# A transformer block's first projection on the unnormed rows, with the norm's factor applied as its tiles leave PSUM

## The reference

```python
xn = rms_norm(h, norm_mix_pre[i])
z = xn @ w_in[i]
z_rwkv, z_gla = z[..., :RWKV_IN_WIDTH], z[..., RWKV_IN_WIDTH:]
...
qkv = jax.nn.silu(centred_dwconv(qkv, conv_w))
...
log_a = jax.nn.log_sigmoid(jnp.einsum('btdr,drc->btdc', a_lo, a_up) + a_b) / GLA_GATE_TEMP
...
o_f = gla_chunked(q_h, k_h, v_h, heads(log_a[:, :, 0], GLA_DK))
```

## Time and profile before

| | us |
|---|---|
| median of 3 runs | 2946.64 (2944.94 to 2954.29) |
| the profiled execution, its own time | 2958.57 |
| its span | 2956.7 |
| `load_constants` and `pre_norm` | 0 to 50.3 |
| `gla_project` | 50.3 to 208.8 |
| `gla_mix` | 208.8 to 327.7 |

### The profile page before, as it was taken

The page is one execution under the profiler, slowest core; times in us unless marked ns, Lnnn a source line. Parts: engine busy times, 40 slices in busy tenths (PEclk is TensorE's granted clock), DMA queues, the critical chain, the costliest instruction groups (busy, mean ns, idle before and its releaser), DMA issues.

```text
span 2956.7 us, 57419 instructions
## 1 busy us (share of the span) xinstructions
PE 2761.1 (93%) x24688; PEld 2261.2 (76%) x24688; DVE 1658.5 (56%) x2482; ACT 1220.4 (41%) x2232; POOL 355.9 (12%) x480
## 2 busy tenths in 40 slices
PE   4997899889998999899999999999999989999997
PEld 4776677788885777688888788788887768888876
DVE  5669676445454666556543437675446655654343
ACT  4776665222223454333333345432245433333331
POOL 2000123545440011101000000000001100100000
PEclk9997899899998999999999999999999999999998
DMA  4420344211101434333345232222323433334432
GB/s 142 136 75 3 103 140 166 64 38 40 39 20 37 137 135 164 130 123 125 118 146 177 87 108 92 89 95 94 100 93 128 164 122 131 121 114 152 165 121 86
DMA packets 138461, 319.27 MB, mean 108 GB/s; under 512 B 13344, under 2 KB 40608, under 8 KB 138208
## 3 DMA queue, kind: packets, MB, share of 16 engines
q1 hardware_dynamic: 115344, 236.94, 24.5%
q0 software_dynamic: 22864, 78.66, 7.6%
HBM read 268.23 MB, written 47.19 MB: 107 GB/s over the span
## 4 chain that ended last, share of the span: by engine, by line
PE 61%; DVE 3%; DMA 2%; ACT 1%; issue 1%; SPq 0%; POOL 0%; DVEq 0%; ACTq 0%
PE be_ps L3278 21%; PE be_ps L3204 16%; PE be_ps L3307 16%; PE be_ps L3257 7%; PE be_ps L3329 1%; DMA be_raw<-in_ffn_up 1%; DMA be_raw<-in_ffn_down 1%; PE be_ps L2784 1%; DMA ext<-f_first 1%; PE be_ps L2778 0%; DVE ext L2842 0%; ACT be_whi L3364 0%; PE be_ps L2411 0%; DVE big L2821 0%; DVE be_raw_r L3607 0%
## 5 line engine op out<-in xcount | busy, mean ns | idle before, releaser
L3607 DVE TENSOR_TENSOR be_raw_r<-be_raw,be_whi 128x1024 fp32r<-128x1024 f32 x229 | 280.6, 1225 | 502.0 <-ACT be_whi L3364 501.8
L3364 ACT CAST be_whi<-be_raw 128x1024 fp32r<-128x1024 f32 x229 | 240.2, 1049 | 608.2 <-DMA be_raw<-in_ffn_down 317.7
L3307 PE MATMUL be_ps<-ext_r,be_whi 128*128 128x512 f32 x1152 | 358.1, 392 | 4.6 <-ACT big L3370 4.6
L3278 PE MATMUL be_ps<-ext_r 128*128 128x512 f32 x832 | 280.9, 396 | 10.4 <-ACT be_ps L3425 10.4
L3204 PE MATMUL be_ps<-ext_r,be_whi 128*128 128x512 f32 x896 | 278.9, 393 | 5.8 <-DVE be_raw_r L3607 3.1
L3307 PEld LDWEIGHTS be_ps<-ext_r,be_whi 128*128 128x128 f32 x1152 | 217.6, 189 | 50.5 <-ACT big L3370 5.5
L3278 PE MATMUL be_ps<-mid_r,ext_r 128*128 128x512 f32 x704 | 226.9, 398 | 10.2 <-ACT be_ps L3425 10.2
L3307 PE MATMUL be_ps<-ext_r,be_raw_r 128*128 128x512 f32 x576 | 225.7, 392 | 0.0
L3204 PEld LDWEIGHTS be_ps<-ext_r,be_whi 128*128 128x128 f32 x896 | 166.9, 188 | 45.4 <-DVE be_raw_r L3607 4.2
L3204 PE MATMUL be_ps<-big_r,be_whi 128*128 128x512 f32 x640 | 198.9, 392 | 0.0
L3278 PEld LDWEIGHTS be_ps<-ext_r 128*128 128x128 f32 x832 | 158.2, 190 | 48.0 <-issue 10.8
(11 more groups left out here) (412 smaller groups left out, 5545.6 us busy)
## 6 DMA issues: line engine op xcount, KB each, us to landing
be_raw<-in_ffn_down SPq DMA_DIRECT2D x88, 512.0 KB, 3.4
be_raw<-in_conv_in SPq DMA_DIRECT2D x48, 512.0 KB, 3.3
ext<-f_inner SPq DMA_DIRECT2D x72, 256.0 KB, 3.7
ext<-in_ffn_gate SPq DMA_DIRECT2D x30, 512.0 KB, 5.1
ext<-in_ffn_up SPq DMA_DIRECT2D x30, 512.0 KB, 4.3
gp_ada<-in_ada POOLq DMA_DIRECT2D x24, 512.0 KB, 3.7
rp_ada<-in_ada POOLq DMA_DIRECT2D x24, 512.0 KB, 4.2
be_raw<-in_ffn_gate SPq DMA_DIRECT2D x44, 256.0 KB, 2.8
```

Of the source, the lines that this page charges most:

```text
L3278: mm = pe.matmul(ps[:, bank], part[:, at], x, start=(not seeded and k == 0 and p == 0), stop=(k == 3 and p == 2), skip_group_check=True)
L3307: mm = pe.matmul(ps[:, steps.bank[n, g]], part[:, at], x, start=(i % NPAIR == 0 and u == 0 and p == 0), stop=(i % NPAIR == NPAIR - 1 and u ...
L3364: act.copy(w.hi[:, n % 3], w.raw[:, n % 3]).then_inc(w.hi_ready, 1)
L3607: dve.tensor_tensor(w.lo(n), w.raw[:, n % 3], w.hi[:, n % 3].bitcast(F32), ALU.subtract).then_inc(w.lo_ready, 1)
```

## The change

`load_constants` and `pre_norm` are gone. Their work is in the block of `gla_project`, in class `FirstNorm`. x is loaded in eight pairs of half tiles; `xn_hi` and `xn_lo` are now made of x times the gain, without the token's factor, and the projection's tile 0 starts on them tile by tile. The squares are made by ACT (five of eight tiles) and POOL (three), the factor is made as 128x1024 numbers (`scale`): PE sums with a matrix of ones between the products of tile 1, ACT takes the root, DVE the reciprocal. Every tile of the projection is now taken out of PSUM by DVE, which multiplies it by `scale`; before, ACT did that. The modulation's `per_step` is another tuple. In `gla_mix` POOL gets 32 instructions that add `xn_hi` and `xn_lo`, multiply by `scale` and split the result again, for `rwkv_project`; SP's second weight load waits for them. `k_factor` of `rwkv_project` uses the memory of `scale`.

```diff
-def pre_norm(core, w, source, h, gain, xn_hi, xn_lo, c, acc):
...
+class FirstNorm:
...
+    POOL_SQUARES = {0: (5, 6, 7), 1: (5, 6, 7)}
...
+    def load(self, sp, hf, q):
+        pair = slice(2 * q, 2 * q + 2)
+        sp.dma_start(self.h[:, pair, self.cols(hf)], self.source[:, pair, self.cols(hf)]).then_inc(self.loaded[hf][q], 16)
+    def hi(self, act, hf, m):
+        act.wait_ge(self.loaded[hf][m // 2], 16)
+        act.activation(self.xn_hi[:, m, self.cols(hf)], self.h[:, m, self.cols(hf)], ACT.Copy, scale=self.gain[:, m:m + 1]
+                       ).then_inc(self.hi_done, 1)
+    def lo(self, dve, hf, m):
+        dve.wait_ge(self.hi_done, KD * hf + m + 1)
+        dve.scalar_tensor_tensor(self.xn_lo[:, m, self.cols(hf)], self.h[:, m, self.cols(hf)], self.gain[:, m:m + 1],
+                                 self.xn_hi[:, m, self.cols(hf)].bitcast(F32), ALU.mult, ALU.subtract
+                                 ).then_inc(self.lo_done, 1)
+    def by_act(self, hf):
+        return [m for m in range(KD) if m not in self.POOL_SQUARES[hf]]
+    def slot(self, hf, m):
+        return self.squares[hf][m]
+    def square(self, act, hf, m):
+        act.activation(self.slot(hf, m), self.h[:, m, self.cols(hf)], ACT.Square).then_inc(self.squared, 1)
+    def pool_sum(self, pool, hf):
+        tiles = self.POOL_SQUARES[hf]
+        done = len(tiles) * hf
+        first = self.slot(hf, tiles[0])
+        for i, m in enumerate(tiles):
+            x = self.h[:, m, self.cols(hf)]
+            pool.wait_ge(self.loaded[hf][m // 2], 16)
+            pool.tensor_tensor(self.slot(hf, m), x, x, ALU.mult).then_inc(self.pool_squared, 1)
+            pool.wait_ge(self.pool_squared, done + i + 1)
+            if i:
+                if i > 1:
+                    pool.wait_ge(self.pool_added, (len(tiles) - 1) * hf + i - 1)
+                pool.tensor_tensor(first, first, self.slot(hf, m), ALU.add).then_inc(self.pool_added, 1)
+    def add(self, dve, hf, i):
+        own, n = self.by_act(hf), len(self.by_act(0)) * hf
+        total = self.slot(hf, own[0])
+        if i < len(own):
+            dve.wait_ge(self.squared, n + i + 1)
+            other, out = self.slot(hf, own[i]), total
+        else:
+            dve.wait_ge(self.pool_added, (len(self.POOL_SQUARES[hf]) - 1) * (hf + 1))
+            other, out = self.slot(hf, self.POOL_SQUARES[hf][0]), self.totals[hf]
+        if i > 1:
+            dve.wait_ge(self.added, n + i - 1)
+        dve.tensor_tensor(out, total, other, ALU.add).then_inc(self.added, 1)
+    def sum_up(self, pe, hf, out):
+        pe.wait_ge(self.added, len(self.by_act(0)) * (hf + 1))
+        pe.matmul(out, cst(self.core, "ones"), self.totals[hf], start=True, stop=True).then_inc(self.summed, 1)
+    def root(self, act, hf, sums):
+        act.wait_ge(self.summed, hf + 1)
+        act.activation(self.scale[:, self.cols(hf)], sums, ACT.Sqrt, bias=eps(self.core, EPS_RMS), scale=1.0 / D
+                       ).then_inc(self.rooted, 1)
+    def reciprocal(self, dve, hf):
+        dve.wait_ge(self.rooted, hf + 1)
+        part = self.scale[:, self.cols(hf)]
+        dve.reciprocal(part, part).then_inc(self.scaled, 1)
...
-        modulation = Modulation(core, ctx, "gp", dram_ada, c, mod, 0, (3, 3, 2, 2, 2, 2, 2, 3, 0, 0, 3, 2), 9)
+        modulation = Modulation(core, ctx, "gp", dram_ada, c, mod, 0, (0, 0, 3, 3, 3, 3, 3, 3, 0, 0, 3, 3), 9)
...
+            sp.dma_start(core.vec[:, :], dram_vec).then_inc(norm.vec_loaded, 16)
+            load_weights(0)
+            for hf in two:
+                for q in range(KD // 2):
+                    norm.load(sp, hf, q)
+            load_weights(1)
+            sp.dma_start(core.const[:, :], dram_const[:, 0:N_STAY * P]).then_inc(norm.const_loaded, 16)
...
-            def drain(s):
-                act.wait_ge(filled, s + 1)
-                if is_conv(s):
-                    if s >= 3:
-                        act.wait_ge(mixed, s - 2)
-                    act.copy(edge[:, s % 2, 1:T + 1], acc[:, s % 2]).then_inc(drained, 1)
-                elif s == 0:
-                    act.copy(lora, acc[:, s % 2]).then_inc(drained, 1)
-                else:
-                    act.activation(z[:, place(s)], acc[:, s % 2], ACT.Silu).then_inc(drained, 1)
+            def finish_gate(s):
+                act.wait_ge(drained, s + 1)
+                act.activation(z[:, place(s)], z[:, place(s)], ACT.Silu)
...
-            for s in range(n_tiles + 1):
+            act.wait_ge(norm.vec_loaded, 16)
+            act.activation(c[:, :], core.vec[:, VEC["c"]:VEC["c"] + KD], ACT.Silu).then_inc(norm.c_ready, 1)
+            act.wait_ge(norm.c_ready, 1)
+            act.activation(scale[:, 0:1], c[:, 0:1], ACT.Sqrt, scale=0.0)
+            weights_hi(0)
+            for hf in two:
+                for m in range(KD):
+                    norm.hi(act, hf, m)
+            weights_hi(1)
+            for hf in two:
+                for m in norm.by_act(hf):
+                    norm.square(act, hf, m)
+            weights_hi(2)
+            act.wait_ge(norm.const_loaded, 16)
+            for hf in two:
+                norm.root(act, hf, side[:, hf])
+            for s in range(2, n_tiles + 1):
                 if s + 1 < n_tiles:
                     weights_hi(s + 1)
-                if s == 2:
-                    act.wait_ge(edged, 1)
-                if s:
-                    drain(s - 1)
+                if s >= 2 and not is_conv(s - 1):
+                    finish_gate(s - 1)
...
+            def drain(s, hf=None):
+                part = slice(0, T) if hf is None else norm.cols(hf)
+                out = edge[:, s % 2, 1:T + 1] if is_conv(s) else z[:, place(s)]
+                dve.wait_ge(filled, s + 1)
+                dve.wait_ge(norm.scaled, 2 if hf is None else hf + 1)
+                ins = dve.tensor_tensor(out[:, part], acc[:, s % 2, part], scale[:, part], ALU.mult)
+                if hf != 0:
+                    ins.then_inc(drained, 1)
...
-            for s in range(n_tiles + 1):
+            dve.memset(edge[:, :, :], 0.0).then_inc(edged, 1)
+            dve.wait_ge(norm.vec_loaded, 16)
+            weights_lo(0)
+            for hf in two:
+                for m in range(KD):
+                    norm.lo(dve, hf, m)
+            weights_lo(1)
+            n_adds = len(norm.by_act(0))
+            for i in range(1, n_adds + 1):
+                norm.add(dve, 0, i)
+            for i in range(1, n_adds - 1):
+                norm.add(dve, 1, i)
+            norm.reciprocal(dve, 0)
+            norm.add(dve, 1, n_adds - 1)
+            norm.add(dve, 1, n_adds)
+            dve.wait_ge(norm.scaled, 1)
+            drain(0, 0)
+            weights_lo(2)
+            norm.reciprocal(dve, 1)
+            drain(0, 1)
+            dve.wait_ge(edged, 1)
+            for s in range(2, n_tiles + 1):
                 if s + 1 < n_tiles:
                     weights_lo(s + 1)
-                if s == 0:
-                    dve.memset(edge[:, :, :], 0.0).then_inc(edged, 1)
-                if s == 2:
-                    dve.wait_ge(edged, 1)
+                drain(s - 1)
...
+            for hf in two:
+                norm.pool_sum(pool, hf)
...
+            pe.wait_ge(w.lo_ready, 1)
+            for hf in two:
+                for k in range(KD):
+                    pe.wait_ge(norm.lo_done, hf * KD + k + 1)
+                    for part_w, x in ((w.w_hi, xn_hi), (w.w_hi, xn_lo), (w.w_lo, xn_hi)):
+                        ins = pe.matmul(half(acc[:, 0], hf), part_w[:, 0, k], half(x[:, k], hf),
+                                        start=(k == 0 and part_w is w.w_hi and x is xn_hi),
+                                        stop=(k == KD - 1 and part_w is w.w_lo))
+            ins.then_inc(filled, 1)
+            for s in range(1, n_tiles):
                 pe.wait_ge(w.lo_ready, s + 1)
                 if s >= 2:
                     pe.wait_ge(drained, s - 1)
                 side_products = modulation.of_step(s - 2) if s >= 2 else ()
                 for k in range(KD):
+                    if s == 1 and k in (5, 7):
+                        if k == 5:
+                            pe.wait_ge(norm.const_loaded, 16)
+                        norm.sum_up(pe, (k - 5) // 2, side[:, (k - 5) // 2])
...
+                if s:
+                    sp.wait_ge(renormed, 4 * KD)
...
+        @block.gpsimd
+        def _(pool):
+            for k in range(KD):
+                if k:
+                    pool.wait_ge(renormed, 4 * k)
+                pool.tensor_tensor(row, xn_hi[:, k].bitcast(F32), xn_lo[:, k].bitcast(F32), ALU.add).then_inc(renormed, 1)
+                pool.wait_ge(renormed, 4 * k + 1)
+                pool.tensor_tensor(row, row, scale[:, :], ALU.mult).then_inc(renormed, 1)
+                pool.wait_ge(renormed, 4 * k + 2)
+                pool.tensor_copy(xn_hi[:, k], row).then_inc(renormed, 1)
+                pool.wait_ge(renormed, 4 * k + 3)
```

(1 more changed line is left out.)

182 lines of the change are left out of this document (28 added, 154 removed).

## The result

The changed kernel took **3018.03 us** (median of 4 runs, 3012.40 to 3025.82), the kernel before beside it 2947.86 (4 runs). The ratio is 1.0237, 95% interval 1.0208 to 1.0266: 2.4% slower. Forecast were 3014 in 2975 to 3032, and "slower" with 0.89.

The account below looks back on a forecast made before the run. PE was taken to bound the projection, DVE the mixing. + 13 and + 55 make + 68 us: the profiled 2958.57 becomes 3027, and from the median 2946.64 the forecast is 3014, range 2975 to 3032.

Parts of the forecast that it names:

- The head: Projection's start: POOL's ten instructions cost DVE 8.8 us, yet tile 2 starts at 49 us, where it was 70.5.
- The steps: Projection steps 3 to 7, three modulation tiles each: 18.5 us a step, step 8 at 160 us against 156.55.
- the tail: Projection's end from step 11: late third load, adds, drains and scans take 27 us before `gla_mix`.
- the + 13: Whole projection: `gla_mix` starts at 222 us against 208.8, 13 us later.
- One sign: Projection steps 3 to 7: PE waits for ACT's pace, idle about 5 us a tile.
- The mixing: `gla_mix`: POOL's 32 instructions take turns with DVE's two-input SBUF ones, 62 us less 7 of cover, + 55 us.
- the cast: POOL's cast in `gla_mix`: taken as 1.6 us, between bounds of 0.9 and 2.5.
- The estimate by the whole duration (65): `gla_mix`: each POOL instruction excludes DVE for its whole length, 8 x 9.0 - 7 = 65 us in place of 55.
- Rival 2: `gla_mix`: DVE is served first, POOL runs in gaps and finishes after it; + 28, within the forecast's 0.80.
- Rival 1: `gla_mix`: POOL reads in DVE's shadow and costs nothing; + 13 stays, 2960 us; chance 0.10.
- The sum: Whole kernel: + 13 in the projection and + 55 in the mixing make + 68 us.
- Rival 3: Projection: third load lands in time, step about 13.4 us, total 2980, or 2930 with free mixing; 0.04 in full.

Follow-up runs that it names:

- Experiment 7: Changed kernel with POOL's squares held until all 16 `xn_lo` are made; 3020.69 us in one run, mixing from 215.0 us on.
- Experiment 6: Changed kernel with three buffers for modulation tiles in place of two, six places for sums in place of nine; 3005.81 us in one run.
- (1): Changed kernel without POOL's 32 instructions in the mixing and SP's wait for them; median 2971.54 us, ratio 1.0032, mixing 119.8 us.
- (2): Changed kernel with POOL's 32 mixing instructions replaced by memsets of the scratch row; 2981.94 us in one run, mixing 119.5 us.
- (4): Changed kernel renorming only channel tiles 0 to 3 on POOL, 16 instructions for 32; 3000.09 us in one run, mixing 146.5 us.
- (3): Changed kernel with POOL's 32 mixing instructions replaced by 32 one-input casts of 128x1024; 2999.09 us in one run, mixing 141.9 us.
- experiment 5: Changed kernel with the mixing's 32 POOL instructions given to DVE, four per block; 3007.98 us in one run, mixing 152.4 us.

## Why the prediction was right, step by step

**The head.** Forecast: first `xn_lo` near 8 us, the sixteenth near 28, tile 2 on PE at 49. Measured: 7.75, 27.83, 48.76. Experiment 7 shows that what the sixteen `xn_lo` take beyond 10.9 us is POOL's turns.

**The steps.** Forecast 18.5 us, measured 18.4. Step 3 began at 65.4 in place of 67, step 8 at 157.6 in place of 160, step 10 at 175.9 in place of 179; the tail took 26.4 us in place of 27. So ACT's pace is as said, and the + 13 is + 9.1 through small terms on the same side, of which the way from tile 2 to step 3 is the largest: 16.6 us in place of the 18.3 that I had summed from rows. In that sum Silu stood with its table, 2.3 us; ACT loaded the table (1.28 us at 47.40) while it waited for the convolution anyway. Against the kernel before, step 10 begins only 0.4 us later (175.87 against 175.43) and PE's last tile 1.9 (197.38 against 195.49); the other 7.2 us come behind that, where DVE has the adds of the late third tile, two drains and two scans left.

One sign did not come: PE was not idle some 5 us a tile. In the five steps it was busy 18.39, 16.77, 17.04, 15.93 and 13.30 us of 92.2, which leaves 10.8 us idle and not 25. It lived on its lead, 21.7 us at tile 2 and 0.5 at tile 9 (161.63 against 162.11), and in three of the steps its granted clock was 0.81, 0.91 and 0.82, so that the same products took longer. For the time of the stage this made no difference, since tiles came at ACT's pace.

Experiment 6 shows the wait for the third load as one part (3 us a step, 22 in all); the convolution behind the drain is the other, which no experiment took away. The wait for it grew from 2.98 to 5.15 us: DVE's drain of 1.22 stands ahead of the convolution, and ACT, without its copy of 1.01, is there sooner. That reading is argued from rows. (Of the steps 2 to 7 the last had three modulation tiles before as well.)

**The mixing.** Forecast + 55, measured + 53.2, and by the mechanism named: + 53 goes to nothing with POOL idle (1) and with POOL only writing (2), halves with half the work (4), goes by the length of POOL's instruction (3). The mis-sized term is the cast: I took 1.6 us from bounds of 0.9 and 2.5, it takes 1.11 to 1.38. The lower bound had a false reason, that no engine does this size faster than about 1 us: in the trace of before DVE's L708 takes 0.75, and in experiment 5 its cast 0.69. Additions and product have 2.34 to 2.69, forecast 2.5 and 2.37; that POOL's rows would show as 2.4 plus DVE's 0.5 did not come, they grew by 0.35 at most, and POOL was over after 72 us and not 85. What a turn costs DVE is the instruction less about 0.3, as the earlier trace rows had it. The estimate by the whole duration (65) was weighed against this one on the strength of the Trainium skill (SBUF, "Who interferes with whom"); the trace decides for the shorter one, with 0.42 us become 2.56 beside 2.40 of POOL. Rival 2, DVE winning the turns, would have stretched POOL's rows to the end of the stage; they were over at 289.7, 72 us in. Rival 1, a free mixing, came only with POOL idle or not reading (1 and 2).

**The total.** The sum was 68 and the profiled difference 59.7, so the sum was 8 us too high. That the median of 3018 nevertheless lies above the forecast of 3014 comes from the base: the profiled execution of before was 11.9 us above its median, which I carried over to the changed kernel, and the profiled one of the changed kernel (3018.17) stands on its median. Two errors of 8 and 12 us cancelled to 4. Of the 8, 3.1 lie in the part that no edit touches. The medians themselves differ by 70.2 us, with an interval of some 61 to 78, so they don't tell 68 from 59.7. The mechanisms are shown; that close a hit is partly luck.

**Rival 3** asked for a step under 13.5 us and a free mixing. With three buffers the wait for the load is gone and the step is still 15.3, so the rival's own 13.4 was 1.9 too low: the wait for the convolution stays. The faster kernel came by taking the mixing's work elsewhere and three edits besides.

## What to carry to other kernels

Work handed to POOL is not taken off DVE when both read SBUF: each POOL instruction holds up one of DVE's two-input instructions for nearly its own length, so what counts is POOL's time, not its idle share, and DVE may do the same work for less (33 us against 53 here). Look for such work a place where DVE reads PSUM, or fold it into an instruction that is there anyway, as the drain. Where PE sets a stage, look for its shortest stops as well, above all between small side products: here 0.5 us of waiting went with a loss of 3 us or more by the clock that followed, and the cure was the order of a few instructions on DVE.
